# A transformer step's beginning reordered: two weight slabs by halves, two chunks side by side, the fifth in its own PSUM bank

## What is computed

```python
def rmsnorm(x, g):
    y = x * rsqrt(mean(x * x) + EPS)
    return y * g
hn = rmsnorm(h, norm_mix[0])
z = gelu(hn @ sgu_w_in[0])            # 1024 -> 4096
u, v = split(z, 2)
v = rmsnorm(v, v_norm)
mixed = einsum('gts,bcsgd->bctgd', tril(w_s), chunks_of(v)) + b_s
h = h + (u * mixed) @ w_out
```

## Time and profile before

| | |
|---|---|
| median of 3 runs | 740.75 us (740.6 to 740.77) |
| profiled execution, its own time | 742.02 us |
| its span, from first to last instruction | 740.3 us |
| mean granted TensorE clock | 0.994 |
| busy: PE, PEld | 729.4 us (99%), 713.1 us (96%) |
| busy: DVE, ACT, POOL | 303.6, 408.2, 539.7 us |

### The profile page before, as it was taken

How to read it: one execution, slowest core, us unless ns; L and a number is a source line. 1 busy time by engine, 2 the same in 40 slices (tenths; PEclk the granted TensorE clock), 3 DMA queues, 4 the chain that set the end, 5 groups by cost and what they waited for, 6 DMA issues and landing times.

```text
span 740.3 us, 16759 instructions
## 1 busy us (share of the span) xinstructions
PE 729.4 (99%) x6287; PEld 713.1 (96%) x6287; DVE 303.6 (41%) x757; ACT 408.2 (55%) x743; POOL 539.7 (73%) x256
## 2 busy tenths in 40 slices
PE   8999999999999999999999999999999999999995
PEld 8999999999999999999999888799999999999995
DVE  5435976223333322232488665754232333321002
ACT  6877555455444454555677566555464444444542
POOL 7986678878887888889867121239878887888891
PEclk9999999999999999999999999999999999999998
DMA  8654354656776755566565898316546555555641
GB/s 287 230 185 143 132 182 155 203 187 203 236 240 228 238 188 172 199 201 199 177 250 190 264 382 291 148 59 201 188 151 201 173 192 174 194 174 191 201 150 58
DMA packets 44408, 144.66 MB, mean 195 GB/s; under 512 B 5602, under 2 KB 5858, under 8 KB 44098
## 3 DMA queue, kind: packets, MB, share of 16 engines
q1 hardware_dynamic: 43778, 142.96, 57.4%
q10 hardware_dynamic: 432, 0.57, 0.2%
q0 software_dynamic: 144, 0.40, 0.1%
HBM read 142.42 MB, written 1.48 MB: 194 GB/s over the span
## 4 chain that ended last, share of the span: by engine, by line
PE 98%; DMA 1%; DVE 1%; ACT 0%; DVEq 0%; issue 0%; ACTq 0%
PE ps L1345 30%; PE ps L1346 29%; PE ps L1347 29%; PE ps L1718 1%; PE ps L1694 1%; PE ps L1638 1%; PE ps L1450 1%; DMA h<-xT 1%; PE ps L1630 0%; PE ps L1631 0%; PE ps L1568 0%; PE ps L1698 0%; PE ps L1384 0%; PE ps L1422 0%; PE ps L1421 0%; PE ps L1426 0%
## 5 line engine op out<-in xcount | busy, mean ns | idle before, releaser
L404 POOL TENSOR_TENSOR wlo<-raw,whi 128x1024 fp32r<-128x1024 f32 x221 | 527.2, 2410 | 179.4 <-ACT whi L474 179.3
L1345 PE MATMUL ps<-xhi,whi 128*128 128x264 f32 x1028 | 295.0, 287 | 0.0
L1346 PE MATMUL ps<-xlo,whi 128*128 128x264 f32 x1028 | 291.3, 283 | 0.0
L1347 PE MATMUL ps<-xhi,wlo 128*128 128x264 f32 x1028 | 291.1, 283 | 0.0
L474 ACT ACTIVATE whi<-raw 128x1024 fp32r<-128x1024 f32 x221 | 232.8, 1054 | 51.7 <-PE ps L1347 50.8
L1346 PEld LDWEIGHTS ps<-xlo,whi 128*128 128x128 f32 x1028 | 193.8, 189 | 0.2
L1345 PEld LDWEIGHTS ps<-xhi,whi 128*128 128x128 f32 x1028 | 193.6, 188 | 0.3
L1347 PEld LDWEIGHTS ps<-xhi,wlo 128*128 128x128 f32 x1028 | 192.8, 188 | 0.0
L1345 PE MATMUL ps<-ahi,whi 128*128 128x264 f32 x352 | 100.0, 284 | 0.0
L1347 PE MATMUL ps<-ahi,wlo 128*128 128x264 f32 x352 | 99.9, 284 | 0.0
L1346 PE MATMUL ps<-alo,whi 128*128 128x264 f32 x352 | 99.9, 284 | 0.0
(11 more groups left out here) (255 smaller groups left out, 1131.2 us busy)
## 6 DMA issues: line engine op xcount, KB each, us to landing
raw<-w_stream SPq DMA_DIRECT2D x222, 512.0 KB, 3.3
pg<-pages SPq DMA_DIRECT2D x64, 288.0 KB, 4.3
pg<-w_ukT SPq DMA_DIRECT2D x1, 2048.0 KB, 8.2
pg<-w_uv SPq DMA_DIRECT2D x1, 2048.0 KB, 10.1
y_out<-h SPq DMA_DIRECT2D x4, 264.0 KB, 2.2
h<-xT ACTq DMA_DIRECT2D x2, 264.0 KB, 5.0
h<-xT SPq DMA_DIRECT2D x2, 264.0 KB, 4.8
raw<-w_stream SPq DMA_DIRECT2D x2, 256.0 KB, 4.3
```

What stands on the lines that cost most here:

```text
L404: pool.tensor_tensor(wlo[:, c % RING, :], raw[:, c % RING, :], whi[:, c % RING, :].bitcast(F32), ALU.subtract).then_inc(lo_ready, 1)
L1345: pe.matmul(out, whi_, mhi, start=start, stop=False)
L1346: pe.matmul(out, whi_, mlo, start=False, stop=False)
L1347: return pe.matmul(out, wlo_, mhi, start=False, stop=stop)
```

## The change

- SP's queue now carries, in this order: first half of slab 0, rows 0 and 1 of h, rows 2 and 3, first half of slab 1 (its own semaphore raw_second), second half of slab 0, rows 4 and 5, rows 6 and 7, second half of slab 1, slabs 2 to 4. ACT's queue keeps the gains alone.
- xhi and xlo of the first norm are made as in the later norms, by `gained`: ACT multiplies and rounds h straight into xhi, DVE makes h times gain less xhi in one instruction, from SBUF. The scaled copy in PSUM and XB are gone.
- ACT: first half of slab 0, rows 0 to 3, first half of slab 1, second half of slab 0, rows 4 to 7, second half of slab 1. After the root it splits slab 5 and then loads the table of the gelu.
- Three of the four half-slab subtractions go from POOL to DVE; POOL keeps the second half of slab 1, and waits ahead of it for lo_first 2, lo_ready 1 and hi_ready 2.
- TensorE: WARM is 9; chunks 0 and 1 go side by side: high products of both first halves, low products of both, the same for the second halves. Ahead of each block of chunk 0 stand `held` products (7, 0, 3, 1, 0, 1, 1, 1), 256 columns of whi by whi, that nobody reads. Chunks 2 to 6 put high products ahead of low ones; the norm sum stands in the middle of chunk 3. Chunk 4 goes to bank 7 (EARLY_BANK), DVE scales it in v_chunk(3). Transposes: 0 after chunk 4, 1 and 2 after chunk 5, 3 after 6, 4 after 7, 5 after 8, 6 after 9, 7 and 8 after 10 (TWICE), then as before; ahead of 1 TensorE waits for psum_read 5. The loops of TensorE and, for chunks 4 to 7, of DVE are written out.

```diff
-WARM = 12
+WARM = 9
...
-        XB = (6, 7, 4, 5)
+        EARLY, EARLY_BANK, TWICE = 4, 7, 10
...
             sp.dma_start(raw[:, 0, 0:SLAB // 2], w_stream[0][:, 0:SLAB // 2]).then_inc(raw_first, 16)
-            sp.dma_start(h[:, 2:4, :], xT[:, 2:4, :]).then_inc(h_in[1], 16)
+            load_rows(0)
+            load_rows(1)
+            sp.dma_start(raw[:, 1, 0:SLAB // 2], w_stream[1][:, 0:SLAB // 2]).then_inc(raw_second, 16)
             sp.dma_start(raw[:, 0, SLAB // 2:SLAB], w_stream[0][:, SLAB // 2:SLAB]).then_inc(raw_ready[0], 16)
-            sp.dma_start(h[:, 6:8, :], xT[:, 6:8, :]).then_inc(h_in[3], 16)
-            for c in range(1, RING + 1):
+            load_rows(2)
+            load_rows(3)
+            sp.dma_start(raw[:, 1, SLAB // 2:SLAB], w_stream[1][:, SLAB // 2:SLAB]).then_inc(raw_ready[1], 16)
+            for c in range(2, RING + 1):
                 load(c)
...
-            for c in range(2):
-                for half, (ready, done) in enumerate(((hi_first, lo_first), (hi_ready, lo_ready))):
...
+            pool.wait_ge(lo_first, 2)
+            pool.wait_ge(lo_ready, 1)
+            pool.wait_ge(hi_ready, 2)
+            w = slice(SLAB // 2, SLAB)
+            pool.tensor_tensor(wlo[:, 1, w], raw[:, 1, w], whi[:, 1, w].bitcast(F32), ALU.subtract).then_inc(lo_ready, 1)
...
+            def first_high(m):
                 act.wait_ge(h_in[m // 2], 16)
+                gained("mix0", m)
...
             first_split(0, 0, raw_first, hi_first)
+            for m in range(KD // 2):
+                first_high(m)
+            first_split(1, 0, raw_second, hi_first)
             first_split(0, 1, raw_ready[0], hi_ready)
-            for m in range(4, KD):
+            for m in range(KD // 2, KD):
                 first_high(m)
-            first_split(1, 0, raw_ready[1], hi_first)
             first_split(1, 1, raw_ready[1], hi_ready)
...
-            root("mix0", ACT.Gelu_apprx_tanh)
+            root("mix0")
             split(AHEAD + 2)
+            table(ACT.Gelu_apprx_tanh)
...
+            for m in range(KD // 2):
+                gained("mix0", m, m)
+            first_slab_low(0, 0, hi_first, lo_first)
+            first_slab_low(1, 0, hi_first, lo_first)
+            for m in range(KD // 2, KD):
+                gained("mix0", m, m)
+            first_slab_low(0, 1, hi_ready, lo_ready)
...
             def v_chunk(u_, i):
+                if not isinstance(i, int) or u_ != EARLY:
+                    scaled_v(u_, i)
                 if not isinstance(i, int) or u_ > 0:
                     add_square(NQ["v"], u_ - 1, i, 4)
+                if isinstance(i, int) and u_ == EARLY - 1:
+                    scaled_v(EARLY, i)
                 if not isinstance(i, int) or u_ > 1:
                     vt_lo(u_ - 2, i)
...
+            def held(times):
+                for _ in range(times):
+                    pe.matmul(ps[:, 3, 0:2 * P], whi[:, 0, 0:P], whi[:, 0, 0:2 * P], start=True, stop=True)
...
+            high_products(0, 0, rows_ready)
+            pe.wait_ge(hi_first, 2)
+            high_products(1, 0)
+            for c in range(2):
+                pe.wait_ge(lo_first, c + 1)
+                low_products(c, 0)
+            pe.wait_ge(hi_ready, 1)
+            high_products(0, 1, rows_ready)
+            pe.wait_ge(hi_ready, 2)
+            high_products(1, 1)
+            for c in range(2):
+                pe.wait_ge(lo_ready, c + 1)
+                low_products(c, 1)
...
             high_first(2)
             high_first(3, "mix0")
+            high_first(4, bank=EARLY_BANK)
+            turn_v(0, 0)
+            pe.wait_ge(psum_read, 2)
+            high_first(5)
+            pe.wait_ge(psum_read, EARLY + 1)
+            turn_v(1, 0)
+            turn_v(2, 0)
+            high_first(6)
+            turn_v(3, 0)
+            for c in range(7, KS):
+                main(c, c, KD, x_of)
+                if c <= TWICE:
+                    turn_v(c - 3, 0)
+                if c >= TWICE:
+                    turn_v(c - 2, 0)
```

More of the change, by code:

```diff
@@ L884, in _, with first_slab_low @@
             dve.wait_ge(gains_in, 16)
[L886 to L908, removed]
+            def first_slab_low(c, half, ready, done):
+                dve.wait_ge(ready, c + 1)
+                w = slice(half * SLAB // 2, (half + 1) * SLAB // 2)
+                lo_of(wlo[:, c, w], raw[:, c, w], whi[:, c, w]).then_inc(done, 1)
+            for m in range(KD // 2):
[5 more added lines that the diff above has]
+            first_slab_low(0, 1, hi_ready, lo_ready)
             for m in range(KD):
@@ L918, in vt_lo, with scaled_v, v_chunk @@
                       vthi[:, at].rearrange("p a b -> p (a b)")).then_inc(vtlo_done, 1)
[L920 removed]
+            def scaled_v(u_, i):
                 wait(dve, slab_used, u_ + 1, i, 4)
                 wait(dve, gelu_done, u_ - 1, i, 4)
[L923 removed]
+                scaled(tt[:, u_ % 2, :], EARLY_BANK if isinstance(i, int) and u_ == EARLY else u_ % BANKS, Ra)
+            def v_chunk(u_, i):
+                if not isinstance(i, int) or u_ != EARLY:
+                    scaled_v(u_, i)
                 if not isinstance(i, int) or u_ > 0:
                     add_square(NQ["v"], u_ - 1, i, 4)
+                if isinstance(i, int) and u_ == EARLY - 1:
+                    scaled_v(EARLY, i)
                 if not isinstance(i, int) or u_ > 1:
                     vt_lo(u_ - 2, i)
[L929 removed]
+            for u_ in range(8):
                 v_chunk(u_, 0)
[L931 removed]
+            with dve.Fori(2, KS // 4) as i:
                 for u_ in range(4):
@@ L1395, in _ @@
             pe.wait_ge(hi_first, 1)
-            for b in range(KD // 2):
-                pe.wait_ge(xlo_done, b + 1)
[L1398 to L1404, removed]
@@ L1430, in _, with high_products @@
-            high_first(1)
+            def held(times):
+                for _ in range(times):
+                    pe.matmul(ps[:, 3, 0:2 * P], whi[:, 0, 0:P], whi[:, 0, 0:2 * P], start=True, stop=True)
+            def high_products(c, half, rows=None, bank=None):
+                out = ps[:, c % BANKS if bank is None else bank, 0:T]
+                for b in range(4 * half, 4 * half + 4):
+                    w = slice(b * P, b * P + P)
+                    if rows:
+                        rows(b)
+                    pe.matmul(out, whi[:, c % RING, w], xhi[:, b, :], start=b == 0, stop=False)
+                    pe.matmul(out, whi[:, c % RING, w], xlo[:, b, :], start=False, stop=False)
@@ new lines, in low_products, with rows_ready @@
+            def low_products(c, half, bank=None):
+                out = ps[:, c % BANKS if bank is None else bank, 0:T]
+                for b in range(4 * half, 4 * half + 4):
+                    w = slice(b * P, b * P + P)
+                    last = pe.matmul(out, wlo[:, c % RING, w], xhi[:, b, :], start=False, stop=b == KD - 1)
+                if half:
+                    last.then_inc(slab_used, 1)
+            def rows_ready(b):
+                held((7, 0, 3, 1, 0, 1, 1, 1)[b])
+                pe.wait_ge(xlo_done, b + 1)
@@ new lines, in _, with high_first @@
+            high_products(0, 0, rows_ready)
[11 more added lines that the diff above has]
+                low_products(c, 1)
+            def high_first(c, between=None, bank=None):
+                pe.wait_ge(hi_ready, c + 1)
+                high_products(c, 0, bank=bank)
+                if between:
+                    norm_sum(between)
+                high_products(c, 1, bank=bank)
+                pe.wait_ge(lo_ready, c + 1)
+                low_products(c, 0, bank)
+                low_products(c, 1, bank)
```

58 lines of the change are left out of this document (5 added, 53 removed).

## The result

The changed kernel takes 742.41 us (median of 8 runs, 741.65 to 743.69); beside it the kernel before took 740.75 (8 runs, 740.6 to 741.04). The ratio is 1.0022, interval 1.0012 to 1.0033: slower by about 1.7 us, outside the forecast range. In two later series on two other chips, 26 and 31 executions of the kernel before had medians of 740.76 and 740.70, and the changed kernel, timed in the first of them, 743.28. So the 13 runs of the kernel after spread over 2.6 us (741.65 to 744.28); those of before, on all chips, over 1.2 (740.40 to 741.57), apart from the one profiled execution of 742.02 on which the forecast rests.

What follows compares the result with a forecast made beforehand. TensorE, busy 99% of the span, was taken as the bound. About 3.1 us won in the beginning less 2.0 given back waiting after slab 5 made 1.1 us off the 740.75 median: 739.6 us, range 738.0 to 741.8.

Steps and rivals of the forecast that it cites:

- landing + 2.4: ACT after slab 5 lands: split 0.96 and table load 1.40 us put the first gelu at 22.0.
- gelu + 5.45: TensorE ahead of transposes 1 and 2: goes on 5.45 us after the first gelu, at 27.45, having stood 1.9 us.
- rival 3: TensorE's clock falls again after the new stall, costing 1.7 us: 741.3; chance 0.16.
- Rival 4: DVE's two-input instructions wait for POOL or rows come late; chunks 0 and 1 end at 15: 740.5 to 741; chance 0.05.
- 3.1 won in the beginning: Chunks 0 and 1 on TensorE: both end about 13.1 against 16.18, 3.1 us ahead.
- Rival 1: Slab 5 lands early, so the root sets the first gelu at 20.5; gain 2.6 us, 738.2; chance 0.27.
- The 1.27: Gap between the profiled execution, 742.02 us, and the runs' median, 740.75; the forecast took 1.1 off that median.
- 3.0 us are lost in chunk 0: TensorE's chunk 0 took 5.9 us where chunk 1 took 2.92, so 3.0 us were counted as lost there.
- the gain is 20.7 less the landing of slab 5: Whole kernel: general rule giving the gain in us from the time at which slab 5's load lands.
- bounds 16.4 to 21.2: Slab 5's landing on SP's queue: 16.4 with slab 4's 3.3 us, 21.2 if the queue was full.
- the duration of slab 5's own row: Slab 5's load on SP's queue: issued at 13.1, the same 6.5 us as before, landing at 19.6.
- rival 2: Slab 5 lands late, at 21.2; first gelu 23.6, gain -0.5 us, 741.2; chance 0.15.

Runs made afterwards that it cites:

- first profile: The changed kernel's first profiled execution, no further edit; 741.65 us, the fastest of its eight runs.
- second: The changed kernel profiled once more, no edit; median 743.28 us, ratio 1.0039 against the kernel before.
- second profile of before: The kernel before, unchanged, run and profiled once more; median 740.72 us, profiled span 739.3.
- experiment 6: Changed kernel with the loads of slabs 5 to 8 ahead of all nine constants; 740.28 us, ratio 0.9994 to the kernel before; repeated, 740.08 us.
- experiments 4 and 6: The first of the two: changed kernel with slab 5's load ahead of the four constants in SP's queue; 741.10 us, ratio 1.0009 to the kernel before.

## Why the prediction was wrong

| step | forecast | first profile | second |
|---|---|---|---|
| first rows of h there | 5.3 | 4.6 | 4.7 |
| chunks 0 and 1 end | 13.1 | 13.50 | 13.79 |
| slab 4 issued | 10.8 | 11.35 | 11.63 |
| slab 5 issued | 13.1 | 13.62 | 13.91 |
| slab 5 lands | 19.6 | 20.1 | 21.5 |
| first gelu | 22.0 | 22.58 | 23.96 |
| wait ahead of transposes 1, 2 | 1.9 | 1.63 | 1.63 |
| chunk 6 | 27.8 | 28.45 | 29.82 |

**Right** were the chain and its order: xlo in steps of 0.41 us (1.72 for four, POOL idle from 5.78 to 11.56), the first two chunks done by 13.5 (forecast 13.1), the root at 17.65 (18.05), ACT idle for slab 5, the new wait and what causes it, landing + 2.4 (2.48), gelu + 5.45 for the transposes (5.46). The first rows came even sooner than the bounds 5.1 to 5.7, but ACT then waited 0.84 us for the first half of slab 1, a wait that the prediction does not have. What POOL's new waits are worth no run shows. The clock did not fall again: rival 3 is out. Rival 4 is out: the beginning does what it says. But the "3.1 won in the beginning" are counted from 16.18; an ordinary execution has its first two chunks done at 15.05 (second profile of before), so the change won 1.3 to 1.6 there. Rival 1's working, root first and then 2.35 to the gelu, is what experiment 6 brought about by hand: gelu at 20.93 for its 20.5, and 26.80 + 713.15 = 739.95.

**Wrong, first: "The median of the runs, 740.75, lies 1.27 below it, so the forecast for the median is 740.75 - 1.1".** The 1.27 was taken as a shift of the whole. It was what that one execution lost, above all by the clock's fall (1.0 of it by the second profile), and the median had nothing of it. The same loss stands in the "3.0 us are lost in chunk 0" that the change was to win back. The prediction's own timeline puts chunk 6 at 27.8, and 27.8 + 713.15 = 740.9, not 739.6: a microsecond figure from a timeline must be compared with where an ordinary execution stands, 27.6, not with 28.88. Seen so, its own numbers gave no gain: "the gain is 20.7 less the landing of slab 5" has to read 27.6 - 8.35 = 19.25 less the landing, where 8.35 is what both profiles have from landing to chunk 6. This is 1.3 of the 2.8 us by which the forecast missed.

**Wrong, second: the landing of slab 5, "at 19.6", bounds 16.4 to 21.2.** The issue came 0.5 to 0.8 later, since slab 4's did (11.35 and 11.63 for 10.8; the 2.3 us from one to the other are right, 2.27). Slab 4's load waits for DVE's third half slab, which stands behind ACT's last xhi, and these came at 10.2 for 9.7, behind the wait for slab 1's first half. And "the duration of slab 5's own row" was one draw from a wide spread: the second profile of before has 5.4 for its 6.5, and the kernel after and the variants that leave its queue alone show landings at 20.1, 21.3, 21.4, 21.5 and 22.6, 6.5 to 8.9 us after the issue. The prediction calls the four loads ahead of it small; two of them carry 512 KB each. The median of 742.41 puts, by the constant, chunk 6 at 29.26 and the landing at 20.9, 1.3 later than forecast. That is rival 2, which the first median bears out (and which by its own working would have been 742.5 with the base put right); it had 0.15, and its price was too low by the base. The two steps make 1.3 + 1.3; the other 0.2 is 8.35 for the 8.2 of the forecast and rounding.

**Why slower, and not just no faster:** before, the split of slab 5 stood behind the table load, at 20.53 in the second profile of before, so a landing until then cost nothing; POOL's wlo of the slab was ready at 24.07, chunk 5 began at 24.73, so half a microsecond more would have cost nothing either (an estimate from these rows; no profile of before shows a late slab 5). The change issues the same load 0.5 us sooner (13.62 against 14.13), lands it no sooner (20.1 and 21.5, against 20.6 and 19.6), has TensorE there earlier, and put 1.4 us of table behind it. Undoing that line gives back most of the loss (741.21), taking the constants out of the slabs' way gives back all of it (740.08 to 740.28).

Left open: whether slabs first beats the kernel before. The two series say 0.42 and 0.65 us faster, but both intervals take in 1. Not tried: constants behind slab 9 or 10, or in another engine's queue; why before, whose queue carries the same loads, has a spread of 1.2 us where the kernel after has 2.6 was not traced run by run. And why the same load lands so differently from run to run stays open; that the constants ahead of it are the cause is shown only for the whole (experiments 4 and 6), not for a single run.

## What to carry to other kernels

When a stage is made to end sooner, look at once for what its successor waits for that does not move with it, here a load whose place in the queue did not move, and put the other work of that engine (a table load) ahead of the wait, not behind it. Before a gain is read from one profile, set its own time and mean clock beside the other runs: what that execution alone lost is no loss to win back. And let a forecast go by the absolute point at which the unchanged rest begins, plus the constant rest.

## What the runs showed of the hardware that was not expected

- One and the same 512 KB load, issued at 13.6 to 13.9 us behind four constants (two of them of 512 KB), landed 6.5, 7.6 and 8.9 us later in three executions, and with the slabs in one row the median of four such loads was 4.0 us (issued 11.40 to 18.0). In the first microseconds the first half of slab 1 came at 7.16 in one execution and at 8.43 in another.
- The beginning differs between executions of the same kernel, though the windows of both give the granted clock as 1.00 up to 7.3 us: the 24 instructions of the products of `ones` took 4.28 us in one and 5.49 in the other (from 4.00 to 5.00 us twelve in the first, seven in the second). Only the first stood at 0.50 for the next 3.40 us, after 1.94 us without a product.
- Idle times of TensorE of 1.63 us, in one execution 1.25 and 1.63 within 5 us, were followed by no fall: the granted clock is 1.00 from 24 to 60 us in both profiles of the kernel after, and the mean was 0.995 or more in every run of the experiments.
